# Where VectorE makes the low part of each weight tile in an attention and projection stage: ahead of the turn's evacuation, or at the turn's end

## The reference

```
x = x + 0.5 * swiglu(rmsnorm(x), ffn1)                    # width 2816
p = rmsnorm(x) @ w_in                                     # one projection, cut in columns:
#   attention q (8 heads of 64), k and v (2 heads of 64), HGRN2 q, forward and backward forget,
#   input, output gate (512 each), two branch gates (1024 each)
y_attn = softmax(rope(norm(q)) @ rope(norm(k)).T) @ v     # per head, over all 512 tokens
y_hgrn = two gated linear recurrences in chunks of 32 tokens, one in each direction
x = x + (sigmoid(ga) * (y_attn @ wA) + sigmoid(gb) * (y_hgrn @ wB)) @ w_out
x = x + 0.5 * swiglu(rmsnorm(x), ffn2)
out = rmsnorm(x)
```

## Time and profile before

| | |
|---|---|
| median of 3 runs | 1135.56 us (1135.17 to 1135.84) |
| the profiled execution, its own time | 1135.17 us |
| its span, first to last instruction | 1133.4 us |
| PE busy | 1124.8 us, 99% of the span |
| DVE busy | 628.1 us, 55% |
| ACT busy | 443.8 us, 39% |
| POOL busy | 83.3 us, 7% |
| mean granted TensorE clock | 0.998 |

### The profile page before, as it was taken

How to read it: one execution, slowest core, us unless ns; L and a number is a source line. 1 busy time by engine, 2 the same in 40 slices (tenths; PEclk the granted TensorE clock), 3 DMA queues, 4 the chain that set the end, 5 groups by cost and what they waited for, 6 DMA issues and landing times.

```text
span 1133.4 us, 16606 instructions
## 1 busy us (share of the span) xinstructions
PE 1124.8 (99%) x6359; PEld 911.9 (80%) x6359; DVE 628.1 (55%) x832; ACT 443.8 (39%) x658; POOL 83.3 (7%) x74
## 2 busy tenths in 40 slices
PE   9999999999999999999999999999999999999997
PEld 7888888888888777776788888888888888888886
DVE  6755555563333596646688767656555555542223
ACT  6423232232222544546856655544232323331223
POOL 0000000000000130000143320020000000000000
PEclk9999999999999999999999999999999999999999
DMA  6332322333322434212221212422243333332221
GB/s 199 122 111 77 108 93 93 117 104 102 102 95 74 177 109 129 75 57 84 69 92 56 71 51 92 177 96 93 79 125 120 89 121 107 119 112 93 99 88 75
DMA packets 51650, 114.78 MB, mean 101 GB/s; under 512 B 21904, under 2 KB 25104, under 8 KB 51344
## 3 DMA queue, kind: packets, MB, share of 16 engines
q1 hardware_dynamic: 32752, 105.16, 27.9%
q10 hardware_dynamic: 18848, 8.92, 2.8%
HBM read 105.41 MB, written 4.19 MB: 97 GB/s over the span
## 4 chain that ended last, share of the span: by engine, by line
PE 98%; DMA 1%; DVE 1%; ACT 0%; ACTq 0%; issue 0%; DVEq 0%
PE ps L1195 27%; PE ps L1197 27%; PE ps L1196 27%; PE ps L1221 4%; PE ps L1220 4%; PE ps L1222 4%; PE ps L1321 1%; PE ps L1338 1%; PE ps L1467 1%; PE ps L1443 1%; DMA xT<-xT_dram 0%; PE ps L1460 0%; PE ps L1421 0%; PE ps L1370 0%; DMA raw<-up_dram 0%; PE ps L1410 0%
## 5 line engine op out<-in xcount | busy, mean ns | idle before, releaser
L1195 PE MATMUL ps<-h_hi,w_hi 128*128 128x512 f32 x1024 | 407.2, 398 | 0.3 <-DVE w_lo L781 0.3
L1197 PE MATMUL ps<-h_hi,w_lo 128*128 128x512 f32 x1024 | 399.1, 390 | 0.0
L1196 PE MATMUL ps<-h_lo,w_hi 128*128 128x512 f32 x1024 | 398.7, 389 | 0.0
L781 DVE TENSOR_TENSOR w_lo<-raw,w_hi 128x1024 fp32r<-128x1024 f32 (+2 forms) x190 | 233.3, 1230 | 176.9 <-ACT w_hi L432 171.0
L432 ACT ACTIVATE w_hi<-raw 128x1024 fp32r<-128x1024 f32 (+1 forms) x182 | 194.7, 1080 | 183.8 <-PE ps L1197 71.6
L1195 PEld LDWEIGHTS ps<-h_hi,w_hi 128*128 128x128 f32 x1024 | 192.2, 188 | 55.6 <-issue 15.2
L1196 PEld LDWEIGHTS ps<-h_lo,w_hi 128*128 128x128 f32 x1024 | 192.3, 188 | 41.8 <-issue 2.9
L1197 PEld LDWEIGHTS ps<-h_hi,w_lo 128*128 128x128 f32 x1024 | 192.2, 188 | 40.4
L504 ACT ACTIVATE g_hi<-un 128x512 fp32r<-128x512 f32 (+1 forms) x44 | 27.8, 632 | 219.5 <-DVE un L781 219.5
L781 DVE TENSOR_TENSOR un<-ps,rs 128x512 f32<-128x512 f32 x44 | 30.4, 691 | 97.3 <-PE ps L1197 97.3
L1195 PE MATMUL ps<-g_hi,w_hi 128*128 128x512 f32 x176 | 68.5, 389 | 0.0
(11 more groups left out here) (232 smaller groups left out, 1151.7 us busy)
## 6 DMA issues: line engine op xcount, KB each, us to landing
raw<-up_dram SPq DMA_DIRECT2D x86, 512.0 KB, 3.3
raw<-proj_dram SPq DMA_DIRECT2D x26, 512.0 KB, 3.4
raw<-down_dram SPq DMA_DIRECT2D x16, 704.0 KB, 4.0
raw<-down_dram SPq DMA_DIRECT2D x22, 512.0 KB, 3.2
raw<-gates_dram SPq DMA_DIRECT2D x16, 512.0 KB, 3.3
raw<-branch_dram SPq DMA_DIRECT2D x8, 512.0 KB, 3.3
raw<-wout_dram SPq DMA_DIRECT2D x8, 512.0 KB, 3.2
x_spill_dram<-xT ACTq DMA_DIRECT2D x1, 2048.0 KB, 7.1
```

Source lines behind the costliest of these rows:

```text
L781: return V.tensor_tensor(out, a, b, op)
L1195: T.matmul(ps[:, bank, :], w_hi[:, slot, cols], moving_hi(j), start=start and j == 0, stop=False)
L1196: T.matmul(ps[:, bank, :], w_hi[:, slot, cols], moving_lo(j), start=False, stop=False)
L1197: ins = T.matmul(ps[:, bank, :], w_lo[:, slot, cols], moving_hi(j), start=False, stop=stop and j == tiles - 1)
```

## The change

In turns i = 9 to 25 of the loop over `PROJ`, 17 turns, DVE's `split_lo(base + i + AHEAD)` is moved from behind `attention_step` to the place that it has in the turns before: behind `inverse_sums(q-1)` and ahead of the evacuation of unit i. No instruction is added or removed, and each keeps its waits. Nothing else in the kernel is touched.

```
-                if i != 1 and i < FIRST_ITEM:
+                if i != 1:
                     split_lo(base + i + AHEAD)
...
                 attention_step(i - FIRST_ITEM)
-                if i >= FIRST_ITEM:
-                    split_lo(base + i + AHEAD)
```

## The result

The changed kernel takes 1145.08 us (median of 4 runs, 1144.41 to 1145.23) against 1135.37 us before (1135.09 to 1135.84): a ratio of 1.0084, 95% interval 1.0072 to 1.0095. It is slower, as forecast; 1143.7 had been predicted, range 1141.3 to 1146.5. The profiled execution took 1144.47 us, 9.3 us more than the one before. Over all 37 runs of the changed kernel on record the median is 1144.84 us (1144.03 to 1145.85), 9.5 us more than before.

The account below looks back on a forecast made before the run. PE was taken as the bound, with DVE and ACT closing into a 7.80 us ring against its 6.74; losses of 3.6, 3.5 and 1.4 made 8.5 us on 1135.17, so 1143.7 us, 8-in-10 range 1141.3 to 1146.5.

Parts of the forecast that it names:

- PE was the bound and had nothing to gain: Whole kernel: PE is busy 99% of the span and its waits total 1.9 us, so no gain over 0.2%.
- The ring: Evacuation, transposes, maxima, exponentials, reciprocal, normalization, `split_hi`, `w_lo` follow one another on DVE and ACT: 7.80 us against PE's 6.74.
- 2.5 us of room, then 1.06 us per turn: PE's scores in the edited turns: 2.50 us of lag are free, then PE stands still 1.06 us per turn.
- First stretch: Steps 0 to 8, up to `weighted(0)`: first wait at scores(5), scores(8) at 487.72 instead of 484.12; loss 3.6 us.
- Second stretch: From p(9), the end of step 9's exponentials, to scores(15), which start at 541.91 instead of 538.38: loss 3.5 us.
- exit: At `weighted(1)`, which needs the transposes of step 15: 4.9 us late, a loss of 1.4 us more.
- A free exit with 0.3 us of room to spare: Sigmoids to `gate_evac(g0)`: 2.5 us later against PE, covered by 2.8 us of room before gate unit 2; costs nothing.
- rival 4: Behind `weighted(1)`: sigmoid chain 3.8 to 5.3 us late, gate unit 2 waits, 1 to 2.5 us more; chance 0.12.
- The sum: Whole kernel: 3.6 + 3.5 + 1.4 = 8.5 us more, giving 1143.7 us, 0.75% slower.
- How the wait would look: PE's scores (L1321): about eight new waits for ACT's `prob`, two of some 0.4 us, six of some 1.06.
- The clock (rival 5): New waits drop PE's clock to 1.2 GHz: 5.7 us more per turn, 1149.4 for one, 1189 for eight; chance 0.03.

Follow-up runs that it names:

- e3: The changed kernel with ACT's `split_hi` moved ahead of `normalize_probs(q-1)` in each turn; 1135.36 us against 1135.39 before.
- e6: The changed kernel, but in turns 10 to 25 the `w_lo` ahead of the evacuation is that of unit i+2, a turn older; 1135.45 us against 1135.34 before.
- e4: The changed kernel with `split_lo` in turns 9 to 25 placed between the evacuation and the attention step; 1140.01 us against 1135.39 before.
- e9: The changed kernel with two extra ACT copies between normalizations and `split_hi` in turns 10 to 25; 1160.21 us against 1135.33 before.
- e1: The changed kernel with the move in turns 9 to 17 alone, turns 18 to 25 as before; 1139.17 us against 1135.39 before.
- e2: The changed kernel with the move in turns 18 to 25 alone, turns 9 to 17 as before; 1141.71 us against 1135.39 before.
- e8: The changed kernel with the last turn (i = 25) put back in the old order; 1143.46 us against 1135.34 before.
- e7: The changed kernel with both of PE's score matmuls waiting for both exponentials of the step before; 1144.55 us against 1135.34 before.

## Why the prediction was right

**PE was the bound and had nothing to gain.** Held: no variant is measurably faster than the kernel before.

**The ring, 7.80 us.** Measured 7.82. The link from the accumulator read's end to the reciprocal, which the order of before hid, can be read now: 472.50 to 472.53, 0.03 us as taken. The handover from `w_hi` to `w_lo` stood in none of the rows that the sum named either; it is 475.01 to 475.05, 0.04 for the 0.03 taken. e3 and e6 open the ring at `split_hi`, e4 takes out one link of 0.6, e9 adds 1.04; the time follows each. One reading was off and enters no sum: in the kernel before, `w_hi` had been ready for 3.1 us when `w_lo` began, not some 4 (it ended at 464.04, `w_lo` began at 467.18). That the ring causes the loss is shown, not only argued.

**2.5 us of room, then 1.06 us per turn.** First stretch 3.6 predicted, 3.73 measured. It starts with the lag that fills (no wait in turns 10 to 13) and ends at `weighted(0)`, as e1 and e2 show.

**Second stretch and exit, 3.5 + 1.4 = 4.9.** Measured 5.14, of which 1.42 are the wait for the transposes of step 15. The terms of the two stretches are 0.1 and 0.2 us small; most of these 0.37 us are what 0.02 us per turn in the ring make over 12.5 turns (0.25).

**A free exit with 0.3 us of room to spare.** Held for the changed kernel: these are the rows that answer to the earlier trace rows.

```profile
558.27 0.63 ACT L577 ACTIVATE forget<-forget 128x512 f32<-128x512 f32 x1 [0.59 <-DVE hgate L781]
...
571.43 0.68 DVE L781 TENSOR_TENSOR xT<-ps,rs 128x512 f32<-128x512 f32 x1
...
572.58 0.39 PE L1193 MATMUL ps<-h_hi,w_hi 128*128 128x512 f32 x1
```

The evacuation ends at 572.11, gate unit 2 starts at 572.58: 0.47 us of room. The chain came 11.7 us late and PE 9.2, so it is the 2.5 us later against PE that were predicted. e8 shows the other side of it: with `weighted(1)` 1.5 us earlier and the sigmoid chain not, the same evacuation is late, and 0.9 us are paid, which is rival 4's mechanism.

**The sum.** 8.5 predicted, 8.95 between the marks. 9.3 by the profiled executions and 9.7 by the medians hold besides that 0.34 us of spread ahead of the stage and what runs differ by.

**What was off.** How the wait would look. I expected about eight waits of PE at the scores, two of 0.4 us and six of 1.06; the profile has six of 0.35 to 0.4 on PE, 15 on its weight loads, and longer score rows. I had treated the two heads as one event. Where they are one, in e7, the picture is the predicted one: eight waits, two of 0.44 and 0.34 us and six of 1.00 to 1.02. The cost was right in the changed kernel because the second head sets it (e7), the picture was not.

**The clock (rival 5)** did not come: the granted clock in 430 to 565 us is 1.00 in the changed kernel. Its price was also too high: in e9, where the clock does fall, it is low for some 3 us at a time and not for a whole turn, see the last section.

## What to carry to other kernels

Idle time on a helper engine is free only for work whose input is already there. Before moving work into it, follow the engines' waits around once: if the moved step waits for another engine's newest result, two engines that ran side by side become one ring, and its length against the bound engine's turn is what decides. Then ask for the room before the first wait and for what resets the lag; that gives the number of turns that pay. To get such a step earlier for nothing, give it an older unit (e6) or make its producer first (e3).

## What the runs showed of the hardware

In e9 PE rests longer at the scores (1.41 us idle, and head by head), and there the granted clock falls for a while, which it never does in the changed kernel with 0.35 us idle or in e7 with 1.02. Timeline of PE and two stretches:

```profile
456.72 0.39 PE L1198 MATMUL ps<-h_hi,w_lo 128*128 128x512 f32 x1
458.51 1.79 PE L1322 MATMUL ps<-qk 64*128 64x512 f32 x4 [1.41 <-ACT prob L560]
460.24 0.53 PE L1196 MATMUL ps<-h_hi,w_hi 128*128 128x512 f32 x1
...
461.85 0.63 PE L1197 MATMUL ps<-h_lo,w_hi 128*128 128x512 f32 x1
462.27 0.63 PE L1198 MATMUL ps<-h_hi,w_lo 128*128 128x512 f32 x1
...
467.51 1.65 PE L1322 MATMUL ps<-qk 64*128 64x512 f32 x4
...
476.23 2.06 PE L1322 MATMUL ps<-qk 64*128 64x512 f32 x4 [1.41 <-ACT prob L560]
```

```profile
460.00:465.00 5.00, 5.00 (x15) 3.77 (x15) 2.29 (x3) 2.68 (x5) 0.00 (x0) 0.66 0.06 6
465.00:470.00 5.00, 5.00 (x20) 3.15 (x19) 2.27 (x8) 3.23 (x8) 0.00 (x0) 1.00 0.28 99
```

Start to start a matmul takes 462.27 - 461.85 = 0.42 us there instead of 0.23, the lower of the clock's two levels, 1.2 GHz; the mean granted clock of those 5 us is 0.66. PE idles for 1.39 to 1.41 us at six of e9's scores, and behind four of them the clock falls, for some 3 us each. It doesn't fall behind the other two (493.95 and 548.35), nor behind the single waits ahead of `weighted(1)` (1.42 us in the changed kernel, 1.92 in e9). So the length of one rest alone doesn't decide it, and what does is not shown.

The section of the Trainium skill that the prediction cited ("TensorE: Matmul & The Clock Gate", "A second HAM failure mode: psum-queue depth-cycling") tells of a clock that swings between its levels with frequent short idle times, and of lost throughput. The swing is seen in e9, the loss is not. The ring sets the turn there, and the slow matmuls fill time in which PE would have waited: behind the fall the next scores (467.51) come with no idle time, 9.00 us after the ones before, and those behind them after 8.72, together two turns of 8.86. The losses are within 0.2 us of those counted at full clock.

Stretches of small matmuls were at times broken by gaps that no engine's semaphore ended: 0.58 us in `weighted(0)` of e2, 0.24 in `weighted(1)` of e7, and in e9 0.19 in `weighted(1)` and 0.41 right behind it. No experiment here looked for their cause, nor for that of the longer `weighted(1)` behind a wait.
